# Expert weights in units of 2 MB instead of 1 MB, with shuffled row copies and a gather for two experts at a time

## The chip, the cores and the metric

One core of a Trainium2 chip runs the kernel. The metric is the device time of one execution, in microseconds (us); less is better.

## The reference

One layer: a mixer (gated linear attention beside a Mamba-2 state-space group) over 16 meta tokens and 256 tokens of width 1024, a LayerNorm, then a mixture of 32 experts, four for each token, and a last LayerNorm. The change is in the mixture, whose blocks hold the tokens of one expert:

```python
logits = (t @ router_w + router_b)
top_v, top_i = lax.top_k(logits, TOP_K)          # 4 of 32
gates = jax.nn.softmax(top_v, axis=-1)
...
xb = t_pad[tok]                                  # the tokens of expert e
hid = clamped_swiglu(xb @ w_gate[e] + b_gate[e], xb @ w_up[e] + b_up[e])
yb = hid @ w_down[e] + b_down[e]
...
out = jax.ops.segment_sum(yb * gate, row_tok)
```

All is float32. Each of w_gate, w_up and w_down is 1024 x 1024 per expert, 4 MB (of 1048576 bytes), so 12 MB per expert and 384 MB in all; every byte is read once.

## The kernel before, in words

The engines' programs are written out by hand, one function per engine, and tied by semaphores. SP issues nearly all loads, in the order of its program.

**Weights.** `ring` holds 16 slots of 1 MB. A unit is 256 rows of one matrix: partition p has rows 2p and 2p+1 side by side, so one partition gets 8 KB that are contiguous in HBM (`unit_src`, L241; `slot`, L248). An expert has 12 units (UPE), in the order w_gate, w_up, w_down. During the mixer the ring holds the 12 units of w_in and four of w_out, in packets of 256 columns (1 KB); as TensorE is through with them (`w_used`, L299), SP fills their slots with expert 0's units and four of expert 1's. Four further units, the w_gate of expert 28, go to the `spare` tiles (`load_spare`, L302) once their places in `arena` are free, and the last round of the ring skips them (`ring_at`, L258). From then on SP waits for each unit until the one 16 before it is used, and issues it (L329). Rounds are of four experts (UNROLL); the rounds between first and last are a loop.

**A tile** is one expert with up to 64 of its tokens (SL). DVE (`select`, L1260) builds `sel`, a 0/1 matrix of tokens by slots, `selG`, the same with the gates' weights, and `oh`. TensorE gathers (`gather`, L930): for each of eight row groups of 128 (`pair_rows`, L254) and two tiles of tokens it multiplies 128 columns of `xh` (as weights, column step two, since rows 2p and 2p+1 lie in one partition) with 64 columns of `sel`. ACT copies the result to `xT`. `hidden` (L947 to L961) multiplies xT with the units of w_gate into bank 4, then w_up into bank 5; the two halves of 512 columns go to two halves of the array. DVE and ACT make the clamped SwiGLU (L1290 to L1299) in `u_c`, TensorE transposes it (L975), and multiplies with w_down (L990). The output goes back to the tokens by `scatter` (L942), with the transposed selG, into banks 0 to 3, which hold the sum over all experts; `start_sums` (L917) begins them with the bias b_down, `add_residual` (L925) adds the residual before the last round. In a tile the first half of the previous tile's scatter stands between w_gate and w_up, then after w_up the gather of the next expert, the transposes of u_c and of selG, and the scatter's second half. Experts with over 64 tokens would get further tiles in a loop at the end; there are none in the profile.

Each `mm` on float32 is two instructions in the profile. The count of a row of TensorE is thus twice that of the code.

Of the kernel before, what the change touches and what calls it, by code (L numbers as in the profile page):

```python
# [8 lines left out]
ALU = mybir.AluOpType  # L9
# [31 lines left out]
RING = 16  # L41
UW = 2048
UPE = 3 * D * FF // (P * UW)
UNROLL = 4
ROUNDS = NE // UNROLL
SPARE = 4
# [9 lines left out]
def build(nc, x, meta, ln_in_g, ln_in_b, w_in, gla_w_a2, gla_b_a, gla_norm_g, ssd_conv_w, ssd_conv_b,  # L56
          ssd_dt_bias, ssd_a_log, ssd_d, ssd_norm_g, w_out, ln1_g, ln1_b, router_w, router_b,
          w_gate, w_up, b_gate, b_up, w_down, b_down, ln2_g, ln2_b, out):
    with ExitStack() as ctx:
# [7 lines left out]
        arena = sb("arena", [P, 19392])  # L67
# [56 lines left out]
        spare = [cut(at, 2, D) for at in (8320, 16576, 3072, 5248)]  # L124
        xT = [cut(at, KT, SL) for at in (2048, 12672)]
# [7 lines left out]
        sel = cut(7808, 2, NT, SL)  # L133
        selGT = cut(10880, SEQ)
# [67 lines left out]
        ln1_in, ln2_in, bias_in, late_in, out_done = sem("ln1_in"), sem("ln2_in"), sem("bias_in"), sem("late_in"), sem("out_done")  # L202
        landed = [sem(f"landed{s}") for s in range(RING)]
# [37 lines left out]
        def unit_src(e, u):  # L241
            m = (w_gate, w_up, w_down)[u // (UPE // 3)]
            q = u % (UPE // 3)
            rows = slice(q * 2 * P, (q + 1) * 2 * P)
            return m[0, e, rows, :].rearrange("(p k) n -> p (k n)", k=2) if isinstance(e, int) else \
                m[0, bass.ds(e, 1), rows, :].rearrange("a (p k) n -> p (a k n)", k=2)

        def slot(s):  # L248
            return ring[:, s, :].rearrange("p (k n) -> p k n", k=2)
# [4 lines left out]
        def pair_rows(v, kt):  # L254

            return v.rearrange("p (q s k) -> p q k s", s=P, k=2)[:, kt // 2, kt % 2, :]
# [10 lines left out]
        def _(sp):  # L267
# [9 lines left out]
            for n, c0 in enumerate(W_ORDER):  # L277
                sp.dma_start(ring[:, n, :].rearrange("p (k n) -> p k n", k=KT),
                             w_in[0, :, c0:c0 + 256].rearrange("(k p) n -> p k n", p=P)).then_inc(landed[n], 16)
# [14 lines left out]
            for n in range(4):  # L294
                sp.dma_start(ring[:, U_OUT + n, :].rearrange("p (k n) -> p k n", k=KT),
                             w_out[0, :, 256 * n:256 * n + 256].rearrange("(k p) n -> p k n", p=P)).then_inc(landed[U_OUT + n], 16)
# [5 lines left out]
            def load_spare(q):  # L302
                sp.dma_start(unit_dst(spare[q]), unit_src(NE - UNROLL, q)).then_inc(spare_in, 16)

            def experts(it):
                first = isinstance(it, int) and it == 0
                for i in range(UPE * UNROLL):
# [6 lines left out]
                    if first and i == U_OUT:  # L314

                        sp.wait_ge(mixT_ps, 4)
                        load_spare(0)
                        sp.wait_ge(bparts_ok, 1)
                        load_spare(1)
                    if first and before < 0:  # L320
                        sp.wait_ge(*w_used[i])
                    else:
                        k, u = before // UPE, before % UPE
                        m, q = u // 4, u % 4
                        if q == 3:
                            sp.wait_ge((g_ps, u_ps, d_ps)[m], it * UNROLL + (k + 1))
                        else:
                            sp.wait_ge(unit_used, (it * UNROLL + k) * 9 + (3 * m + q + 1))
                    sp.dma_start(ring[:, at % RING, :], unit_src(it * UNROLL + i // UPE, i % UPE)).then_inc(landed[at % RING], 16)  # L329
                    if first and i == RING - 1:  # L330
                        sp.wait_ge(logit_ps, 1)
                        load_spare(2)
                        sp.wait_ge(h1_ok, NT)
                        load_spare(3)
# [4 lines left out]
            sp.wait_ge(g_ps, NE - UNROLL + 1)  # L339
# [18 lines left out]
        def _(pool):  # L358
# [54 lines left out]
            for t in range(NT):  # L413
                pool.wait_ge(h1T_ps, 2 * t + 2)
                link(nc.gpsimd.tensor_tensor(xh[:, t, :], xh[:, t, :], lnbc[:, 0, :], ALU.mult))
                nc.gpsimd.tensor_tensor(xh[:, t, :], xh[:, t, :], lnbc[:, 1, :], ALU.add).then_inc(h1_ok, 1)

        @block.scalar
        def _(act):
# [147 lines left out]
            def xT_evac(n, par, done):  # L567

                act.wait_ge(gath_ps, n + 1)
                if done is not None:  # L570
                    act.wait_ge(u_ps, done)
                nc.scalar.activation(xT[par][:, :, :].rearrange("p k s -> p (k s)"), bank[7][:, :], ACT.Copy).then_inc(xT_ok, 1)  # L572

            def tile(n, par, first, ahead):
                act.wait_ge(a_ok, n + 1)
                nc.scalar.activation(s_c, a_c, ACT.Sigmoid, scale=SALPHA).then_inc(sig_ok, 1)  # L576
                if ahead:
                    xT_evac(n + 1, 1 - par, None if first else n)
# [4 lines left out]
                act.wait_ge(selT_ps, n + 1)  # L583
                if not first:
                    act.wait_ge(scat[1], n)
                nc.scalar.activation(selGT, bank[5][:, 0:SEQ], ACT.Copy).then_inc(selGT_ok, 1)

            xT_evac(0, 0, None)
            for k in range(UNROLL):
                tile(k, k % 2, k == 0, True)  # L590
            with act.Fori(1, ROUNDS - 1) as it:
                for k in range(UNROLL):
                    tile(it * UNROLL + k, k % 2, False, True)
            for k in range(UNROLL):
                tile(NE - UNROLL + k, k % 2, False, k < UNROLL - 1)
            act.wait_ge(list_ok, 1)
            nx = act.value_load(xcount[0:1, 0:1], min_val=0, max_val=MAXX)
            with act.If(nx > 0):
                with act.Fori(0, nx) as i:
                    xT_evac(i + NE, 0, i + NE)  # L600
                    tile(i + NE, 0, False, False)
# [7 lines left out]
        def _(pe):  # L609
# [9 lines left out]
            def wslot(n, kt, a=0, b=256):  # L619
                return ring[:, n, :].rearrange("p (k n) -> p k n", k=KT)[:, kt, a:b]  # L620
# [32 lines left out]
            for c in range(XC):  # L653
                n = U_XBC + c // 2
                pe.wait_ge(landed[n], 16)
# [30 lines left out]
            pe.wait_ge(landed[U_K], 16)  # L686
# [15 lines left out]
            pe.wait_ge(landed[U_V], 16)  # L702
# [28 lines left out]
            pe.wait_ge(landed[U_V + 1], 16)  # L731
# [25 lines left out]
            pe.wait_ge(landed[U_Q], 16)  # L757
# [36 lines left out]
            for hf in range(2):  # L794
                n = U_Z + hf
                pe.wait_ge(landed[n], 16)
# [45 lines left out]
            for hf in range(2):  # L842
                n = U_OG + hf
                pe.wait_ge(landed[n], 16)
# [12 lines left out]
            def out_part(t, kts, first):  # L857
                for nb in range(2):
                    b = bank[((1, 4), (2, 3))[t][nb]]
                    for kt in kts:  # L860
                        ins = mm(b[:, :], mixT[:, kt, t * P:(t + 1) * P],  # L861
                                 ring[:, U_OUT + 2 * nb:U_OUT + 2 * nb + 2, kt * 256:(kt + 1) * 256],
# [4 lines left out]
            for n in range(4):  # L867
                pe.wait_ge(landed[U_OUT + n], 16)
# [51 lines left out]
            def add_residual():  # L920

                pe.wait_ge(residual_ok, 1)
                for t in range(NT):
                    for h in range(2):
                        mm(bank[2 * t + h][:, :], residual[:, :], xh[:, t, h * 512:(h + 1) * 512], start=False, stop=False,  # L925
# [11 lines left out]
            def scatter(n, t):  # L937
# [3 lines left out]
                for h in range(2):  # L941
                    ins = mm(bank[2 * t + h][:, :], selGT[h * SL:(h + 1) * SL, t * P:(t + 1) * P], y_s[h * SL:(h + 1) * SL, :],  # L942
# [3 lines left out]
            def tile(n, par, first, unit_at, arrived, gathers, scatters):  # L946

                def hidden(m, b, free, done):
# [5 lines left out]
                    for q in range(4):  # L954
                        arrived(4 * m + q)
                        for k in range(2):
                            kt = 2 * q + k
                            for h in range(2):
                                ins = mm(b[h * SL:(h + 1) * SL, :], xT[par][:, kt, :], unit_at(4 * m + q)[:, k, h * 512:(h + 1) * 512],  # L959
                                         start=False, stop=kt == KT - 1)  # L960
                        ins.then_inc(done if q == 3 else unit_used, 1)  # L961

                pe.wait_ge(selG_ok, n + 1)
                pe.wait_ge(xT_ok, n + 1)
                hidden(0, bank[4], a_ok, g_ps)
                if scatters:
# [411 lines left out]
```

## Time and profile before

| | |
|---|---|
| median of 3 runs | 1138.41 us (1137.51 to 1139.66) |
| the profiled execution | 1139.48 us |
| its span, first to last instruction | 1137.6 us |
| mean granted TensorE clock | 0.984 |
| TensorE (PE) busy | 1095.9 us, 96% |
| VectorE (DVE) / ScalarE (ACT) / GpSimd (POOL) busy | 231.1 / 123.7 / 30.7 us |
| DMA | 426.96 MB, 375 GB/s over the span |

The time of an execution contains the span and some 2 us around it. The page cuts the span in 40 slices of 28.4 us; digits are tenths busy. "PEld" is the load of TensorE's weights, which overlaps matmuls. In the chain of waits each piece is what the end was waiting for at that time. A matmul's end is modelled, so that consecutive rows of TensorE are best compared by their starts.

### The profile page before, as it was taken

To read this page: it belongs to the slowest core of one execution; us is meant where nothing else is said; L and a number is where in the kernel's file an instruction comes from. 1 tells how busy PE (TensorE), PEld (TensorE's weight loads), DVE (VectorE), ACT (ScalarE), POOL (GpSimd) and SP (SyncE) were. 2 spreads that over 40 slices of the span, in tenths; PEclk is the share of its full clock that TensorE was granted. 3 is DMA by queue.
4 is the path that set the end of the run, shared out by engine and by line. 5 is a ranking of instruction groups with operands and counts; after the bars stand their busy time and mean duration, and the time that the engine had idled before them with its cause. 6 is when DMAs were issued, how large, how long until landed. Compare 5 with 4: busy or idle time off the path is not lost.

```text
span 1137.6 us, 13806 instructions
## 1 busy us (share of the span) xinstructions
PE 1095.9 (96%) x5600; PEld 517.9 (46%) x5600; DVE 231.1 (20%) x528; ACT 123.7 (11%) x250; POOL 30.7 (3%) x37
## 2 busy tenths in 40 slices
PE   6999998999999999999999999999999999999994
PEld 5787756444444444444444433333333333344441
DVE  4422464011111111111111111111111111111114
ACT  2241422000000000000000000000000000000001
POOL 0230002000000000000000000000000000000000
PEclk9989997899999999999999999999999999999998
DMA  8973534899999999999999999999999999999992
GB/s 260 353 302 125 170 150 157 349 411 422 421 421 420 421 421 422 421 422 421 422 422 422 422 422 422 421 423 421 422 421 423 421 422 422 422 422 421 422 419 87
DMA packets 78240, 426.96 MB, mean 375 GB/s; under 512 B 10537, under 2 KB 27026, under 8 KB 29058
## 3 DMA queue, kind: packets, MB, share of 16 engines
q1 hardware_dynamic: 76082, 423.83, 91.4%
q10 hardware_dynamic: 2128, 2.70, 0.9%
q8 instruction: 22, 0.36, 0.1%
q14 instruction: 8, 0.07, 0.0%
HBM read 425.46 MB, written 1.05 MB: 375 GB/s over the span
## 4 chain that ended last, share of the span: by engine, by line
PE 66%; DMA 29%; DVE 2%; ACT 2%; SPq 1%; issue 0%; DVEq 0%
DMA ring<-in_moe_w_up 28%; PE bank L959 26%; PE bank L990 13%; PE bank L934 7%; PE bank L942 4%; PE bank L659 3%; PE bank L861 2%; PE bank L847 1%; PE bank L799 1%; SPq L329 1%; PE bank L953 1%; PE bank L975 1%; PE bank L735 1%; PE bank L675 1%; PE bank L761 1%; PE bank L682 0%
## 5 line engine op out<-in xcount | busy, mean ns | idle before, releaser
L959 PE MATMUL bank<-ring,arena 128*64 128x512 f32 x2016 | 452.7, 596 | 13.6 <-DMA ring<-in_moe_w_up 13.6
L959 PEld LDWEIGHTS bank<-ring,arena 128*64 128x64 f32 x2016 | 139.7, 137 | 294.4 <-issue 234.5
L990 PE MATMUL bank<-ring,arena 128*64 128x512 f32 x1024 | 231.1, 604 | 0.0
L990 PEld LDWEIGHTS bank<-ring,arena 128*64 128x64 f32 x1024 | 71.7, 139 | 156.2 <-issue 137.0
L934 PEld LDWEIGHTS bank<-arena 128*128 128x128 f32 x1024 | 126.2, 200 | 25.1 <-issue 25.1
L934 PE MATMUL bank<-arena 128*128 128x64 f32 x1024 | 130.4, 287 | 0.0
L1303 DVE COPY arena<-bank 128x512 f32<-128x512 f32 x32 | 22.1, 692 | 346.3 <-PE bank L990 346.3
L1294 DVE TENSOR_SCALAR arena<-bank 128x512 f32<-128x512 f32 x32 | 22.1, 692 | 261.9 <-PE bank L959 261.9
L942 PE MATMUL bank<-arena 64*128 64x512 f32 x256 | 72.2, 642 | 0.9 <-DVE arena L1303 0.9
L576 ACT ACTIVATE arena<-arena 128x512 f32<-128x512 f32 x32 | 20.2, 631 | 465.8 <-DVE arena L1290 465.8
L1290 DVE TENSOR_SCALAR arena<-bank 128x512 f32<-128x512 f32 x32 | 22.1, 692 | 186.9 <-PE bank L959 186.9
L572 ACT ACTIVATE arena<-bank 128x512 f32<-128x512 f32 x32 | 19.1, 598 | 362.1 <-PE bank L934 362.1
L942 PEld LDWEIGHTS bank<-arena 64*128 64x128 f32 x256 | 19.4, 184 | 32.5 <-issue 32.5
L659 PE MATMUL bank<-arena,ring 128*128 128x272 f32 x128 | 30.4, 393 | 0.7 <-ACT arena L436 0.7
L861 PE MATMUL bank<-ring,arena 128*128 128x512 f32 x64 | 27.9, 593 | 0.9 <-ACT arena L430 0.9
L953 PE MATMUL bank<-arena 96*64 96x512 bf16 x128 | 25.7, 396 | 0.8 <-ACT arena L572 0.8
L659 PEld LDWEIGHTS bank<-arena,ring 128*128 128x128 f32 x128 | 23.8, 190 | 5.5 <-ACT arena L436 0.9
L975 PE MATMUL bank<-ident,arena 128*128 128x128 f32 x128 | 21.7, 292 | 2.2 <-DVE arena L1299 2.2
L1299 DVE SCALAR_TENSOR_TENSOR arena<-arena 128x512 f32<-128x512 f32 x32 | 22.2, 693 | 3.3
L953 PEld LDWEIGHTS bank<-arena 96*64 96x64 bf16 x128 | 7.3, 108 | 34.0 <-issue 34.0
L1296 DVE TENSOR_TENSOR arena<-arena 128x512 f32<-128x512 f32 x32 | 21.8, 681 | 0.0
L975 PEld LDWEIGHTS bank<-ident,arena 128*128 128x128 f32 x128 | 19.1, 218 | 3.1 <-DVE arena L1299 3.1
(242 smaller groups left out, 527.0 us busy)
## 6 DMA issues: line engine op xcount, KB each, us to landing
ring<-in_moe_w_up SPq DMA_DIRECT2D x128, 1024.0 KB, 26.2
ring<-in_moe_w_down SPq DMA_DIRECT2D x128, 1024.0 KB, 26.3
ring<-in_moe_w_gate SPq DMA_DIRECT2D x124, 1024.0 KB, 25.7
ring<-in_w_in SPq DMA_DIRECT2D x12, 1024.0 KB, 11.9
ring<-in_w_out SPq DMA_DIRECT2D x4, 1024.0 KB, 13.7
arena<-in_moe_w_gate SPq DMA_DIRECT2D x4, 1024.0 KB, 4.7
arena<-in_x SPq DMA_DIRECT2D x2, 512.0 KB, 4.7
arena<-in_ln_in_g SPq DMA_DIRECT2D x1, 512.0 KB, 10.0
```

The costliest lines, as they stand in the source:

```text
L659: ins = mm(bank[4 + c % 3][:, 3:3 + TOK], wslot(n, kt, (c % 2) * P, (c % 2) * P + P), hT[:, kt, :], start=kt == 0, stop=kt == KT - 1)
L861: ins = mm(b[:, :], mixT[:, kt, t * P:(t + 1) * P], ring[:, U_OUT + 2 * nb:U_OUT + 2 * nb + 2, kt * 256:(kt + 1) * 256], start=first and k ...
L934: ins = mm(bank[7][:, kt * SL:(kt + 1) * SL], pair_rows(xh[:, t, :], kt), sel[:, par, t, :], start=t == 0, stop=t == 1)
L942: ins = mm(bank[2 * t + h][:, :], selGT[h * SL:(h + 1) * SL, t * P:(t + 1) * P], y_s[h * SL:(h + 1) * SL, :], start=False, stop=False, ski ...
L953: mm(b[h * SL:(h + 1) * SL, :], oh[:, par, :], bparts[:, m, h * 512:(h + 1) * 512], start=True, stop=False)
L959: ins = mm(b[h * SL:(h + 1) * SL, :], xT[par][:, kt, :], unit_at(4 * m + q)[:, k, h * 512:(h + 1) * 512], start=False, stop=kt == KT - 1)
L975: ins = tr(bank[4][:, c * P:(c + 1) * P], pair_rows(u_c, c), ident[:, :])
L990: ins = mm(bank[6][h * SL:(h + 1) * SL, :], hidT[:, kt % 4, (kt // 4) * SL:(kt // 4 + 1) * SL], unit_at(8 + q)[:, k, h * 512:(h + 1) * 512 ...
L1290: ts(a_c, bank[4][:, :], LIMIT, None, ALU.min).then_inc(a_ok, 1)
L1294: ts(u_c, bank[5][:, :], LIMIT, -LIMIT, ALU.min, ALU.max).then_inc(u_ok, 1)
L1299: stt(u_c, u_c, 1.0, a_c, ALU.add, ALU.mult).then_inc(hid_ok, 1)
L1303: copy(y_s, bank[6][:, :]).then_inc(yd_ok, 1)
```

## The change

A unit becomes 512 rows of one matrix, 2 MB: partition p has rows 4p to 4p+3, 16 KB contiguous in HBM. The ring has 8 such slots, an expert 6 units (two per matrix). The spares are six pieces of 1 MB (8 KB in a partition) instead of four: w_gate and half of w_up of expert 28, the first in a place of its own and loaded at once behind w_out.

With four rows per partition, a row group would take every fourth column. To keep the step at two, POOL writes the normalised tokens to a new tile `h1p` in a shuffled order (per block of 512: two halves, each with two neighbours of four), and DVE writes `a_c` and `u_c` in the same order. `add_residual` reads h1p back in natural order.

The gather is made for two experts at once: `sel` has 64 columns of each, and a gather of 4 row groups with 128 columns stands in each of two tiles: tile n makes half of what experts n+2 and n+3 (n even) or n+1 and n+2 (n odd) need. The halves go to `xA` (two buffers) and `xB`. So both halves for experts 0 and 1 come first, and experts 30 and 31 gather nothing. The transposes of selG move ahead of w_up and into bank 6, `selGT` gets two buffers, the scatter's first half moves behind w_up, and start_sums ahead of w_up. The scratch for descriptors that software makes shrinks to 1024 bytes, which gives room in SBUF.

```diff
-RING = 16
-UW = 2048
+RING = 8
+UW = 4096
+HW = UW // 2
+RPP = UW // FF
 UPE = 3 * D * FF // (P * UW)
+UPM = UPE // 3
-SPARE = 4
+SPARE = 3
...
-        arena = sb("arena", [P, 19392])
+        arena = sb("arena", [P, 19392 + NT * D + HW])
...
-        spare = [cut(at, 2, D) for at in (8320, 16576, 3072, 5248)]
-        xT = [cut(at, KT, SL) for at in (2048, 12672)]
+        h1p = cut(19392, NT, D)
+        spare = [cut(at, 2, D) for at in (19392 + NT * D, 8320, 16576, 3072, 5248, 0)]
+        xA = [cut(at, 4, 2 * SL) for at in (2048, 11648)]
+        xB = cut(12672, 4, 2 * SL)
...
-        sel = cut(7808, 2, NT, SL)
-        selGT = cut(10880, SEQ)
+        sel = cut(7808, NT, 2 * SL)
+        selGT = [cut(at, SEQ) for at in (10880, 16320)]
...
+            m, q = (w_gate, w_up, w_down)[u // UPM], u % UPM
+            rows = slice(q * RPP * P, (q + 1) * RPP * P)
+            return m[0, e, rows, :].rearrange("(p k) n -> p (k n)", k=RPP) if isinstance(e, int) else \
...
+        def shuffled(v):
+            return v.rearrange("p (q a s k) -> p q a s k", a=2, s=P, k=2)
+        def natural(v):
+            return v.rearrange("p (q s a k) -> p q a s k", a=2, s=P, k=2)
+        def row_group(v, kt):
+            return shuffled(v)[:, kt // RPP, kt % RPP // 2, :, kt % 2]
...
-            w_used = [(conv_ps, 2), (conv_ps, 4), (conv_ps, 6), (conv_ps, 8), (k_ps, 1), (v_ps, 3), (v_ps, 3), (q_ps, 1),
-                      (half_used, 1), (z_ps, 2), (half_used, 2), (og_ps, 2), (wout_ps, 3), (wout_ps, 3), (wout_ps, 4), (wout_ps, 4)]
+            w_used = [((conv_ps, 4),), ((conv_ps, 8),), ((k_ps, 1), (v_ps, 3)), ((q_ps, 1),), ((z_ps, 2),), ((og_ps, 2),),
+                      ((wout_ps, 3),), ((wout_ps, 4),)]
+            load_spare(0)
...
-                nc.gpsimd.tensor_tensor(xh[:, t, :], xh[:, t, :], lnbc[:, 1, :], ALU.add).then_inc(h1_ok, 1)
+                for q in range(2):
+                    ins = nc.gpsimd.tensor_tensor(shuffled(h1p[:, t, :])[:, q, :, :, :], natural(xh[:, t, :])[:, q, :, :, :],
+                                                  natural(lnbc[:, 1, :])[:, q, :, :, :], ALU.add)
+                ins.then_inc(h1_ok, 1)
...
-            def gather(n, par):
-                pe.wait_ge(sel_ok, n + 1)
-                for kt in range(KT):
+            def gather(g, pair, half, b):
+                pe.wait_ge(sel_ok, pair + 1)
+                for k in range(4):
                     for t in range(NT):
-                        ins = mm(bank[7][:, kt * SL:(kt + 1) * SL], pair_rows(xh[:, t, :], kt), sel[:, par, t, :], start=t == 0, stop=t == 1)
+                        ins = mm(b[:, k * P:(k + 1) * P], row_group(h1p[:, t, :], 4 * half + k), sel[:, t, :], start=t == 0, stop=t == 1)
                 ins.then_inc(gath_ps, 1)
...
-                ts(u_c, bank[5][:, :], LIMIT, -LIMIT, ALU.min, ALU.max).then_inc(u_ok, 1)
+                ts(shuffled(u_c)[:, 0, :, :, :], natural(bank[5][:, :])[:, 0, :, :, :], LIMIT, -LIMIT, ALU.min, ALU.max).then_inc(u_ok, 1)
```

**TensorE, the tile of expert 1.** In these names L953 and L982 are the bias of w_gate and w_up, L959 and L988 those matrices, L942 and L971 half a scatter, L934 and L963 the gather, L975 and L1009 the transposes of u_c, L978 and L997 those of selG, L990 and L1020 w_down. Before:

```order
L953 MATMUL bank<-arena 64x512 x2
L959 MATMUL bank<-ring,arena 64x512 x16
L942 MATMUL bank<-arena 128x512 x2
L953 MATMUL bank<-arena 64x512 x2
L959 MATMUL bank<-ring,arena 64x512 x16
L934 MATMUL bank<-arena 128x64 x16
L975 MATMUL bank<-ident,arena 128x128 x4
L978 MATMUL bank<-ident,arena 128x128 x2
L942 MATMUL bank<-arena 128x512 x2
L990 MATMUL bank<-ring,arena 64x512 x16
```

and now:

```order
L982 MATMUL bank<-arena 64x512 x2
L988 MATMUL bank<-ring,arena 64x512 x16
L997 MATMUL bank<-ident,arena 128x128 x2
L982 MATMUL bank<-arena 64x512 x2
L988 MATMUL bank<-ring,arena 64x512 x16
L971 MATMUL bank<-arena 128x512 x2
L963 MATMUL bank<-arena 128x128 x8
L1009 MATMUL bank<-ident,arena 128x128 x4
L971 MATMUL bank<-arena 128x512 x2
L1020 MATMUL bank<-ring,arena 64x512 x16
```

The gather has half the instructions at twice the columns; the selG transposes and half a scatter have changed sides of w_up.

**TensorE, the last tile** from its bias of w_up on (the same names). Before:

```order
L953 MATMUL bank<-arena 64x512 x2
L959 MATMUL bank<-ring,arena 64x512 x16
L975 MATMUL bank<-ident,arena 128x128 x4
L978 MATMUL bank<-ident,arena 128x128 x2
L942 MATMUL bank<-arena 128x512 x2
L990 MATMUL bank<-ring,arena 64x512 x16
```

and now, where the tile before it (expert 30) reads the same:

```order
L982 MATMUL bank<-arena 64x512 x2
L988 MATMUL bank<-ring,arena 64x512 x16
L971 MATMUL bank<-arena 128x512 x2
L1009 MATMUL bank<-ident,arena 128x128 x4
L971 MATMUL bank<-arena 128x512 x2
L1020 MATMUL bank<-ring,arena 64x512 x16
```

Without a gather, half a scatter is all that stands between w_up and the transposes, in two tiles now.

**SP, from the loads of w_out to the end of expert 1's units** (L303 and L322 are the spares). Before:

```order
L295 DMA ring<-in_w_out 128x8x256 x4
L329 DMA ring<-in_moe_w_gate 128x2048 x4
L329 DMA ring<-in_moe_w_up 128x2048 x4
L329 DMA ring<-in_moe_w_down 128x2048 x4
L303 DMA arena<-in_moe_w_gate 128x2048 x2
L329 DMA ring<-in_moe_w_gate 128x2048 x4
L303 DMA arena<-in_moe_w_gate 128x2048 x2
L329 DMA ring<-in_moe_w_up 128x2048 x4
L329 DMA ring<-in_moe_w_down 128x2048 x4
```

and now:

```order
L315 DMA ring<-in_w_out 128x8x256 x4
L322 DMA arena<-in_moe_w_gate 128x2048
L351 DMA ring<-in_moe_w_gate 128x4096 x2
L351 DMA ring<-in_moe_w_up 128x4096 x2
L351 DMA ring<-in_moe_w_down 128x4096 x2
L322 DMA arena<-in_moe_w_gate 128x2048 x2
L351 DMA ring<-in_moe_w_gate 128x4096 x2
L322 DMA arena<-in_moe_w_gate 128x2048
L322 DMA arena<-in_moe_w_up 128x2048 x2
L351 DMA ring<-in_moe_w_up 128x4096 x2
L351 DMA ring<-in_moe_w_down 128x4096 x2
```

Half as many issues of twice the size, and two more pieces to the spares.

## Rows read from the trace of the kernel before

**Rows 1.** The page: GB/s in 40 slices, and the packets.
```profile
GB/s 260 353 302 125 170 150 157 349 411 422 421 421 420 421 421 422 421 422 421 422 422 422 422 422 422 421 423 421 422 421 423 421 422 422 422 422 421 422 419 87
DMA packets 78240, 426.96 MB, mean 375 GB/s; under 512 B 10537, under 2 KB 27026, under 8 KB 29058
```

**Rows 2.** The page: the chain that ended last, by engine and by line.
```profile
PE 66%; DMA 29%; DVE 2%; ACT 2%; SPq 1%; issue 0%; DVEq 0%
DMA ring<-in_moe_w_up 28%; PE bank L959 26%; PE bank L990 13%; PE bank L934 7%; PE bank L942 4%; PE bank L659 3%; PE bank L861 2%; PE bank L847 1%; PE bank L799 1%; SPq L329 1%; PE bank L953 1%; PE bank L975 1%; PE bank L735 1%; PE bank L675 1%; PE bank L761 1%; PE bank L682 0%
```

**Rows 3.** The chain in order of time: start, duration, what.
```profile
340.26 6.87 PE bank L959 x32
...
368.33 6.87 PE bank L959 x32
...
467.68 3.91 PE bank L934 x32
...
843.86 27.01 DMA ring<-in_moe_w_up
...
903.49 27.01 DMA ring<-in_moe_w_up
```

**Rows 4.** Timeline of TensorE, expert 27: start, duration, instruction, idle before.
```profile
992.66 1.94 PE L959 MATMUL bank<-ring,arena 128*64 128x512 f32 x8 [0.55 <-DMA ring<-in_moe_w_up]
994.53 3.98 PE L934 MATMUL bank<-arena 128*128 128x64 f32 x32
998.35 0.68 PE L975 MATMUL bank<-ident,arena 128*128 128x128 f32 x4
998.86 0.38 PE L978 MATMUL bank<-ident,arena 128*128 128x128 f32 x2
999.17 1.13 PE L942 MATMUL bank<-arena 64*128 64x512 f32 x4
1000.23 7.09 PE L990 MATMUL bank<-ring,arena 128*64 128x512 f32 x32
```

**Rows 5.** Timeline of SP's queue: the first refills, and the first of w_down's slots.
```profile
196.92 5.48 SPq L329 DMA_DIRECT2D ring<-in_moe_w_up  x4
...
221.51 6.62 SPq L329 DMA_DIRECT2D ring<-in_moe_w_gate  x4
```

**Rows 6.** Windows: stretch, busy us by engine, granted clock, DMA share, GB/s.
```profile
30.00:46.00 16.00, 16.00 (x78) 13.22 (x77) 8.25 (x16) 2.98 (x11) 3.05 (x4) 1.00 1.10 348
300.00:900.00 600.00, 590.82 (x3045) 246.55 (x3044) 91.35 (x209) 44.63 (x84) 0.00 (x0) 1.00 1.01 422
188.00:192.00 4.00, 4.00 (x21) 4.00 (x21) 0.00 (x0) 0.00 (x0) 0.00 (x0) 0.50 0.00 0
216.00:224.00 8.00, 8.00 (x20) 2.17 (x20) 0.00 (x0) 0.00 (x0) 0.00 (x0) 0.57 0.47 177
224.00:232.00 8.00, 8.00 (x40) 2.64 (x38) 1.69 (x6) 0.00 (x0) 0.00 (x0) 1.00 0.99 361
```

**Rows 7.** Timeline of all engines, from the second LayerNorm to the first gather.
```profile
168.22 2.13 PE L617 MATMUL bank<-ident 128*128 128x128 f32 x18
...
178.44 2.35 POOL L416 TENSOR_TENSOR arena<-arena 128x1024 f32<-128x1024 f32 x1
...
184.65 0.42 DVE L1271 TENSOR_SCALAR arena<-arena 128x64 f32<-128x64 f32 x2
...
185.57 6.93 PE L934 MATMUL bank<-arena 128*128 128x64 f32 x32
```

**Rows 8.** The page's costliest groups: the gather's weight loads, count, busy us, mean ns.
```profile
L934 PEld LDWEIGHTS bank<-arena 128*128 128x128 f32 x1024 | 126.2, 200 | 25.1 <-issue 25.1
```

**Rows 9.** Timeline of TensorE, the last expert, from w_up on.
```profile
1103.60 7.03 PE L959 MATMUL bank<-ring,arena 128*64 128x512 f32 x32
...
1112.83 0.75 PE L975 MATMUL bank<-ident,arena 128*128 128x128 f32 x4 [2.19 <-DVE arena L1299]
...
1115.00 8.51 PE L990 MATMUL bank<-ring,arena 128*64 128x512 f32 x32
```

More of the change, by code:

```diff
@@ L202, in build @@
         ln1_in, ln2_in, bias_in, late_in, out_done = sem("ln1_in"), sem("ln2_in"), sem("bias_in"), sem("late_in"), sem("out_done")
+        w_landed = [sem(f"w_landed{n}") for n in range(16)]
         landed = [sem(f"landed{s}") for s in range(RING)]
@@ L963, in tile @@
                 pe.wait_ge(selG_ok, n + 1)
-                pe.wait_ge(xT_ok, n + 1)
-                hidden(0, bank[4], a_ok, g_ps)
-                if scatters:
-                    scatter(n - 1, 0)
+                hidden(0, bank[4], hidT_ok, g_ps)
+                if not first:
+                    pe.wait_ge(yd_ok, n)
+                for t in range(NT):
+                    ins = tr(bank[6][:, t * P:(t + 1) * P], selG[:, par, t, :], ident[:, :])
+                ins.then_inc(selT_ps, 1)
@@ L968, in tile @@
                 if first:
+                    start_sums()
                     pe.wait_ge(list_ok, 1)
                 hidden(1, bank[5], u_ok, u_ps)
-                if gathers:
-                    gather(n + 1, 1 - par)
+                if scatters:
+                    scatter(n - 1, 0, 1 - par)
+                if gathers is not None:
+                    gather(*gathers, bank[7])
                 pe.wait_ge(hid_ok, n + 1)
                 for c in range(4):
-                    ins = tr(bank[4][:, c * P:(c + 1) * P], pair_rows(u_c, c), ident[:, :])
+                    ins = tr(bank[4][:, c * P:(c + 1) * P], row_group(u_c, c), ident[:, :])
@@ L1002, in arrived @@
                         if at is None:
-                            pe.wait_ge(spare_in, 16 * SPARE)
+                            pe.wait_ge(spare_in, 16 * 2 * SPARE)
                         else:
-                            pe.wait_ge(landed[at % RING], it * (UPE * UNROLL // RING * 16) + (2 + at // RING) * 16)
+                            pe.wait_ge(landed[at % RING], it * (UPE * UNROLL // RING * 16) + (1 + at // RING) * 16)
                     n = it * UNROLL + k
-                    first, last = (isinstance(n, int) and n == m for m in (0, NE - 1))
-                    tile(n, k % 2, first, unit_at, arrived, not last, not first)
+                    first = isinstance(n, int) and n == 0
+                    ahead = not (isinstance(n, int) and n >= NE - 2)
+                    pe.wait_ge(xT_ok, n + 2 if ahead else NE)
+                    tile(n, k % 2, first, unit_at, arrived, k // 2,
+                         (n + 2, it * (UNROLL // 2) + (k // 2 + 1), k % 2) if ahead else None, not first)
             pe.wait_ge(h1_ok, NT)
-            gather(0, 0)
+            gather(0, 0, 0, bank[7])
+            pe.wait_ge(GT_ok, 1)
+            gather(1, 0, 1, bank[6])
             pe.wait_ge(bparts_ok, 1)
@@ L1019, in _ @@
             for t in range(NT):
[L1020 removed]
+                scatter(NE - 1, t, 1)
             pe.wait_ge(list_ok, 1)
@@ L1284, in _, with tile @@
             copy(xcount, rank[:, 3 * NE - 1:3 * NE]).then_inc(list_ok, 1)
-            def tile(n, par, first, after):
+            def tile(n, par, first, after, pair):
+                if pair is not None:
+                    select(n + 2, pair)
                 if after is not None:
-                    select(None if first else n, after, 1 - par)
+                    weigh(None if first else n, after, 1 - par)
                 dve.wait_ge(g_ps, n + 1)
-                ts(a_c, bank[4][:, :], LIMIT, None, ALU.min).then_inc(a_ok, 1)
+                ts(shuffled(a_c)[:, 0, :, :, :], natural(bank[4][:, :])[:, 0, :, :, :], LIMIT, None, ALU.min).then_inc(a_ok, 1)
                 dve.wait_ge(u_ps, n + 1)
```

202 lines of the change are left out of this document (105 added, 97 removed).

## The prediction

> **What bounds the kernel now.** Read the page first. The rate of the DMA engines is the flattest line on it: 421 to 423 GB/s from the eleventh slice to the thirty-eighth [rows 1], while TensorE looks just as full. The two can't both be the limit, so the chain of waits comes next: 28% of the span is a wait for a w_up unit, and TensorE has 66% [rows 2]. In order of time it has three parts. Early, the w_gate phase of one expert starts 28.07 us after the last (340.26 to 368.33): TensorE's own pace. From about 635 us the chain is DMA, and two experts take 903.49 - 843.86 = 59.63 us, 29.82 us each [rows 3]. At 994.53 us, when the last w_up unit of expert 27 is used, it goes back to TensorE, because expert 28 finds its w_gate in the spare units [rows 4].
>
> Why does the rate not fall while TensorE sets the pace? An expert needs 12.58 MB. At 28.07 us that is 448 GB/s, more than DMA delivers; the full 16 MB ring is being eaten up and is empty at 635 us. So from 221.5 us on, when SP issues the first refill of a w_down unit [rows 5], transfers never stop, and what counts is **rate x bytes up to expert 27's last w_up, then TensorE's work after it**. Faster work of TensorE before that point only empties the ring sooner.
>
> **The packet.** From 300 to 900 us packets of 8 KB (two rows of 4 KB in a partition) run at 422 GB/s; from 30 to 46 us the w_in packets of 1 KB run at 348 [rows 6]. For one of 16 engines that is 310.6 ns for 8 KB and 47.1 ns for 1 KB. A line through both: 9.4 ns for each packet, and 36.8 ps per byte (27.2 GB/s per engine, 435 for 16). A 16 KB packet would take 9.4 + 602.3 = 611.7 ns, 428.5 GB/s. One MB (1048576 bytes) then takes 2.447 us where it took 2.485.
> The Trainium skill (DMA: Bandwidth & Descriptors, Specifications) gives 435 GB/s as the ceiling of the ports into SBUF, which is where my line ends; its HBM limit per core there, about 358 GB/s, is refuted by the 422 of this trace, and by it longer packets would gain nothing.
>
> **The change, part by part.** Everything is against the profiled execution: 1137.6 us of span in 1139.48 us, the runs' median 1138.41.
> 1. *Longer packets.* Units 24 to 331 (counted in MB from the first expert) pass between 221.5 us and expert 27's last w_up: 308 MB x (2.485 - 2.447) = **-11.7 us**. Bounds: 0 (the rate of 8 KB stays), and 308 x (2.485 - 2.410) = -23 us with no overhead at all. I take the line, since it comes out of two rates of this queue.
> 2. *When the stream becomes dense.* This is the first w_down release of expert 0. Sel for two experts adds two DVE operations of 64 columns, +0.4 us, ahead of the first gather [rows 7]. Both first gathers together have 32 instructions, as the 6.93 us of now, 217 ns each at half the clock; with 128 columns at most twice the 118 of a transpose (5), 236 ns or +0.6 us, and I take nothing. In tile 0 the gather is half, -1.95 us (see 5), of which the DVE chain to hid_ok takes back 0.2. The first release comes after 2 MB, not 1: 1.75 us more at full clock, and with the granted clock at 0.57 from 216 to 224 us [rows 6] up to 3.4. The four matmuls with b_down only move from behind the transposes to ahead of w_up. Together +1.8 us (range 0.4 to 2.7). Against it, the 1 MB refills ran dry while TensorE was slow: 361 GB/s from 224 to 232 us [rows 6], which is 1.2 us lost; two 2 MB refills bridge this. Net **+0.7 us**, with -0.8 to +2.7 as bounds.
> 3. *The last w_up unit is twice as large.* After it lands TensorE has 16 instructions instead of 8, 3.6 us instead of the 1.9 from 992.66 [rows 4]: **+1.7 us**.
> 4. *From there to expert 27's w_down.* Before, 994.53 to 1000.23 [rows 4]. Now the transposes of selG (998.86 to 999.17, 0.31 us) stand ahead of w_up, the first half of the scatter (1.06 us, 999.17 to 1000.23) comes here from ahead of w_up, and the gather has 16 instructions of 128 columns instead of 32 of 64.
> 5. *The gather's price.* The 32 take 3.82 us until the transposes (994.53 to 998.35) and 3.9 on the chain, 122 ns each [rows 3, 4]. A weight load of 128x128 is recorded with 200 ns, but they overlap [rows 8]; a matmul of 64 columns is the shorter part of the pair. With 128 columns behind each load there are 18 transposes in 2.13 us, 118 ns each [rows 7]. So 16 x 122 ns = 1.95 us, a gain of 1.95. Worst: 16 x 200 = 3.2, a gain of 0.7. I take 1.95, as the transposes have the same load and the same columns. Term 4 is then -1.95 - 0.3 + 1.06 = **-1.2 us**.
> 6. *Experts 28 to 31, TensorE's pace.* 28 and 29 still gather: -1.95 each; the part moved inside a tile nets to nothing. 30 no longer gathers, and now waits for DVE's chain as 31 does: w_down came 5.7 us after w_up with a gather and 4.4 without (1110.63 to 1115.00) [rows 9], so -1.3, -0.3 for the selG transposes that stood there, and -0.75 for 0.31 instead of 1.06 between w_gate and w_up: -2.3. Expert 31: -0.3 and -0.75, -1.05. Sum **-7.3 us**. It holds only if DMA isn't behind: expert 27's last w_up lands at 992.6 - 11.7 + 0.7 = 981.6; the 4 MB of its w_down and the 42 left take 46 x 2.447 = 112.6 us, to 1094.2. TensorE's last w_down ends at 1115.0 + 8.5 - 17.8 = 1105.7 and wants its last 2 MB 3.5 us before, at 1102.2: 8 us of cover. The two more MB in spares are 4.9 of these 8 and earn nothing else.
> 7. *Costed at nothing.* POOL writes t=1's rows in two strided pieces of 512; it ended at 180.8 and the gather started at 185.57 [rows 7], so even twice the 2.35 us is hidden; without that cover it costs its own excess. w_in and w_out land in halves of slots, same bytes. The first fill waits for two units' users, but DMA stands idle from 188 to 192 us and on to 196.92, when the first refill is issued [rows 5, 6]. DVE's two strided writes read PSUM in pairs: before 635 us they lie under the gather and the scatter, in 30 and 31 not; 10% more is 0.1 us. After the last w_down nothing changes.
>
> Sum: -11.7 + 0.7 + 1.7 - 1.2 - 7.3 = **-17.8 us**, so 1138.4 - 17.8 = **1120.6 us**.
>
> **Rivals.** A measurement of this kernel can tell about 0.2%, 2.3 us.
> *A, the packets bring no rate.* Either the 3% between 422 and 435 is not per packet, or the queue cuts a row of 16 KB in two. For it: only two points make the line, and the packets of 1 KB are strided reads. Against: 422 is the same in TensorE's part and in DMA's, so nothing but the transfers themselves sets it. Then the sum is -6.1: 1132.3 us, faster by TensorE's end alone.
> *B, long reads are slower.* Packets that are under way at the same time lie twice as far apart in HBM; if they then get in each other's way, the rate falls. In -6.1 + 308 x d the sum passes +2.3 at d = 0.027 us per MB, that is under 417.4 GB/s; at 413 (2.539) it is -6.1 + 16.6 = +10.5, 1149 us. For it: the 1 KB reads of w_in also lay apart by whole rows of w_in and were slow, which the line lays to their size alone. Against: the unit as a whole is as contiguous as before.
> [...]
> *C, TensorE's clock falls in new gaps.* At 1115 us w_down took 8.51 us against 7.09 after a gap of 2.2 us [rows 4, 9]. Tiles 30 and 31 now both have a gap, but of 1.1 us, as half a scatter stands in it. Two falls: +1.4 us on mine, 1122; none: 1119.2. It is inside the forecast.
> *D, partly.* A third or two thirds of the rate: 1124 to 1129.
>
> **How the numbers follow.** Forecast with C 0.66 (the line through two rates is good evidence, the trace has no 16 KB packet); A 0.18; D 0.10; B and any other unseen loss, such as a queue that runs dry with eight slots, 0.06. The range must take in A, and below it the no-fall case and a somewhat better rate: 1116 to 1133.5. The forecast's own range is 1117 to 1124. A and D are still faster by over 0.2% (1136.1). So faster 0.93, same 0.03, slower 0.04.
>
> **What would show it.** Packets of 8 KB and more fall by half, from 78240 - 29058 = 49182 [rows 1]. The windows from 300 to 900 us read 428, not 422; DMA waits on the chain start earlier: the ring's lead lasted 414 us at a loss of 1.75 us per expert, and at 29.4 - 26.1 = 3.3 it ends near 430 us. Matmuls of the gather take 122 ns each, half as many. After expert 27's last w_up the chain is TensorE alone, in tiles of 26.1. A rate of 422 with this end speaks for A, one under 418 for B; DMA waits in experts 28 to 31 would refute term 6.

## The result and the profile after

The changed kernel takes 1120.09 us (median of 4 runs, 1117.96 to 1121.48) against 1137.96 us beside it (4 runs, 1136.51 to 1139.66): ratio 0.9841, 95% interval 0.9819 to 0.9862. Forecast were 1120.6 us and a range from 1116.0 to 1133.5. Run again later (e9), the ratio was 0.9839 (0.9815 to 0.9863).

The first profile has a span of 1116.2 us in an execution of 1117.96 us, the quickest of the four, while the profile of the kernel before lies among its slow ones (1139.48 us). The two spans are thus 21.4 us apart, the medians 17.9. Its GB/s and packets, as in [rows 1], and the chain, as in [rows 2], on the page:

```profile
GB/s 260 353 319 151 129 164 237 312 426 426 428 427 426 429 427 428 429 427 429 429 429 428 428 428 430 428 429 428 428 429 427 429 429 429 428 428 428 428 427 103
DMA packets 51022, 426.93 MB, mean 382 GB/s; under 512 B 7513, under 2 KB 24002, under 8 KB 26034
...
PE 54%; DMA 40%; DVE 3%; ACT 2%; issue 1%; DVEq 0%; SPq 0%
```

TensorE is still 93% busy, and still isn't the bound: DMA has gone from 29 to 40% of the chain. 51022 - 26034 = 24988 packets of 8 KB or more moved what 49182 did. The windows, to set beside [rows 6]:

```profile
184.00:196.00 12.00, 10.50 (x63) 7.57 (x63) 4.49 (x22) 2.85 (x4) 0.00 (x0) 0.86 0.37 154
216.00:224.00 8.00, 7.27 (x36) 3.24 (x38) 0.00 (x0) 1.02 (x2) 0.00 (x0) 1.00 0.95 377
300.00:900.00 600.00, 561.50 (x2722) 209.54 (x2720) 92.21 (x212) 41.72 (x84) 0.00 (x0) 1.00 1.01 428
```

428 GB/s where 422 stood. And the chain in order of time (start, duration, what), as [rows 3]:

```profile
409.10 6.89 PE bank L988 x32
416.01 34.16 DMA ring<-in_moe_w_up
...
590.94 35.41 DMA ring<-in_moe_w_up
...
679.03 35.41 DMA ring<-in_moe_w_up
...
943.31 35.41 DMA ring<-in_moe_w_up
```

The chain goes over to DMA at 416 us, not at 635. From there a step of 679.03 - 590.94 = 88.09 us is three experts (36 MB): 2.447 us per MB, 29.36 per expert. The end of that stretch, on TensorE's timeline, as [rows 4]:

```profile
978.77 3.65 PE L988 MATMUL bank<-ring,arena 128*64 128x512 f32 x16 [1.24 <-DMA ring<-in_moe_w_up]
982.35 1.13 PE L971 MATMUL bank<-arena 64*128 64x512 f32 x4
983.41 2.15 PE L963 MATMUL bank<-arena 128*128 128x128 f32 x16
985.40 0.63 PE L1009 MATMUL bank<-ident,arena 128*128 128x128 f32 x4
985.96 1.13 PE L971 MATMUL bank<-arena 64*128 64x512 f32 x4
987.02 7.09 PE L1020 MATMUL bank<-ring,arena 128*64 128x512 f32 x32
994.03 3.89 PE L953 MATMUL bank<-arena,tri 128*128 128x512 f32 x8
997.86 0.41 PE L982 MATMUL bank<-arena 96*64 96x512 bf16 x2
...
1017.30 7.09 PE L1020 MATMUL bank<-ring,arena 128*64 128x512 f32 x32
...
1043.65 7.09 PE L1020 MATMUL bank<-ring,arena 128*64 128x512 f32 x32
...
1095.00 7.09 PE L1020 MATMUL bank<-ring,arena 128*64 128x512 f32 x32
```

After 978.77 there is no wait for DMA up to the end, as in the kernel before. The difference of the spans, 1137.6 - 1116.2 = 21.4 us, falls to these stretches, each from a start to a start:

| stretch | before | after | difference | forecast |
|---|---|---|---|---|
| to the first w_down refill (SP) | 221.51 | 221.06 | -0.5 | +1.8 |
| from there to the last w_up of expert 27 | 771.2 | 757.7 | -13.4 | -11.7 - 1.2 |
| that unit's matmuls, to the next work | 1.9 | 3.6 | +1.7 | +1.7 |
| to expert 27's w_down | 5.7 | 4.7 | -1.0 | -1.2 |
| to expert 31's w_down | 114.8 | 108.0 | -6.8 | -7.3 |
| from there to the end | 22.6 | 21.2 | -1.4 | 0 |

In the profile of e9, an execution of 1121.45 us, the same rows come to +2.4, -12.8, then +0.7 for the next two together, -6.8 and -1.4, in all -17.9 us: between these two profiles the first row moves by 2.9 us, the second by 0.6 and the others by less than 0.1.

### The profile page after: what moved, and what is told of

Same layout as the page of the kernel before. It is cut to its first block, busy times and chain, and to the rows that moved or that the text cites. A ratio compares the mean times of both kernels' runs of the same rounds, so it can differ in the third digit from the quotient of the medians.

```text
span 1116.2 us, 12278 instructions
## 1 busy us (share of the span) xinstructions
PE 1040.0 (93%) x5088; PEld 457.1 (41%) x5088; DVE 231.6 (21%) x528; ACT 119.6 (11%) x250; POOL 31.9 (3%) x39
## 2 busy tenths in 40 slices
DMA packets 51022, 426.93 MB, mean 382 GB/s; under 512 B 7513, under 2 KB 24002, under 8 KB 26034
## 4 chain that ended last, share of the span: by engine, by line
PE 54%; DMA 40%; DVE 3%; ACT 2%; issue 1%; DVEq 0%; SPq 0%
DMA ring<-in_moe_w_up 22%; PE bank L988 20%; DMA ring<-in_moe_w_gate 18%; PE bank L1020 12%; PE bank L963 3%; PE bank L971 3%; PE bank L687 3%; PE bank L889 2%; PE bank L875 1%; PE bank L827 1%; PE bank L1009 1%; PE bank L763 1%; PE bank L982 1%; PE bank L789 1%; PE bank L703 1%
## 5 line engine op out<-in xcount | busy, mean ns | idle before, releaser
L988 PE MATMUL bank<-ring,arena 128*64 128x512 f32 x2000 | 452.0, 598 | 45.6 <-DMA ring<-in_moe_w_up 34.5
L988 PEld LDWEIGHTS bank<-ring,arena 128*64 128x64 f32 x2000 | 139.1, 137 | 328.1 <-issue 239.4
L1020 PE MATMUL bank<-ring,arena 128*64 128x512 f32 x1024 | 226.8, 595 | 0.7 <-issue 0.7
L1020 PEld LDWEIGHTS bank<-ring,arena 128*64 128x64 f32 x1024 | 71.1, 137 | 151.9 <-issue 151.9
L963 PEld LDWEIGHTS bank<-arena 128*128 128x128 f32 x512 | 64.0, 200 | 23.3 <-issue 23.3
L971 PE MATMUL bank<-arena 64*128 64x512 f32 x256 | 72.0, 640 | 0.9 <-DVE arena L1351 0.9
L963 PE MATMUL bank<-arena 128*128 128x128 f32 x512 | 69.9, 291 | 0.2 <-DVE arena L1310 0.2
L598 ACT ACTIVATE arena<-bank 128x512 f32<-128x512 f32 x32 | 19.1, 597 | 326.5 <-PE bank L963 326.5
L971 PEld LDWEIGHTS bank<-arena 64*128 64x128 f32 x256 | 19.4, 184 | 31.0 <-issue 27.3
L982 PE MATMUL bank<-arena 96*64 96x512 bf16 x128 | 25.7, 396 | 0.7 <-issue 0.7
L1009 PE MATMUL bank<-ident,arena 128*128 128x128 f32 x128 | 20.5, 283 | 2.4 <-DVE arena L1347 2.3
L612 ACT ACTIVATE arena<-bank 128x512 f32<-128x512 f32 x32 | 19.0, 593 | 18.0 <-PE bank L1009 18.0
L1009 PEld LDWEIGHTS bank<-ident,arena 128*128 128x128 f32 x128 | 17.7, 202 | 4.2 <-DVE arena L1347 4.2
## 6 DMA issues: line engine op xcount, KB each, us to landing
ring<-in_w_in SPq DMA_DIRECT2D x12, 1024.0 KB, 11.7
```

The lines of the kernel that those rows point to most:

```text
L963: ins = mm(b[:, k * P:(k + 1) * P], row_group(h1p[:, t, :], 4 * half + k), sel[:, t, :], start=t == 0, stop=t == 1)
L971: ins = mm(bank[2 * t + h][:, :], selGT[par][h * SL:(h + 1) * SL, t * P:(t + 1) * P], y_s[h * SL:(h + 1) * SL, :], start=False, stop=False ...
L982: mm(b[h * SL:(h + 1) * SL, :], oh[:, par, :], bparts[:, m, h * 512:(h + 1) * 512], start=True, stop=False)
L988: ins = mm(b[h * SL:(h + 1) * SL, :], (xA[pp], xB)[q][:, k, par * SL:(par + 1) * SL], unit_at(UPM * m + q, k)[:, h * 512:(h + 1) * 512], s ...
L1009: ins = tr(bank[4][:, c * P:(c + 1) * P], row_group(u_c, c), ident[:, :])
L1020: ins = mm(bank[6][h * SL:(h + 1) * SL, :], hidT[:, kt % 4, (kt // 4) * SL:(kt // 4 + 1) * SL], unit_at(2 * UPM + q, k)[:, h * 512:(h + 1) ...
```

## The experiments

All kernels below are the changed kernel with the edit shown. e1 to e4, e5 to e8, and e9 with e10 ran together, each group on one chip and beside its own runs of the kernel before. Differences to the changed kernel therefore go by ratios where nothing else is said.

### Is it the packet?

The theory is the line of the prediction: 9.4 ns per packet and 36.8 ps per byte on each of 16 engines. Three kernels change the packet (the spares stay at 8 KB), and with it the number of transfers: two or four for a unit, or one for two units. A fourth changes the number of transfers alone.

**e1_packets_8k**, and with `PARTS = 4` **e2_packets_4k**:

```diff
-                    sp.dma_start(ring[:, at % RING, :], unit_src(...)).then_inc(landed[at % RING], 16)
+                    for j in range(PARTS):                       # 2; part j: rows 4p+2j, 4p+2j+1
+                        w = UW // PARTS
+                        sp.dma_start(ring[:, at % RING, j * w:(j + 1) * w], part_src(..., j)).then_inc(landed[at % RING], 16)
...
```

> The changed kernel, but each ring unit of 2 MB is loaded by two DMAs of 8 KB per partition (rows 4p, 4p+1, then 4p+2, 4p+3). Slots, waits, layout and TensorE's work stay. Theory (a fixed price per packet): the windows from 300 to 900 us fall from 428 back to 422 GB/s, 2.485 us per MB, and the time rises by 308 x 0.038 = 11.7 us, to 1131.8. Rival (the gain of rate comes from fewer, larger units): 428 GB/s stays, 1120. Packets of 8 KB and more go back to about 49 thousand by both.

> As the one with packets of 8 KB, but four DMAs of 4 KB per partition for each ring unit. The line through 1 KB and 8 KB gives 9.4 + 150.6 = 160.1 ns per packet, 409 GB/s from 300 to 900 us and 2.561 us per MB: 308 x 0.114 = +35 us on the change, 1155. Rival (1 KB was slow for its strides and there is no price per packet from 4 KB on): 422 GB/s or more, at most 1132.

**e4_packets_32k**, a whole matrix into two slots, outside the last round:

```diff
+                    if paired:
+                        sp.dma_start(ring[:, (at - 1) % RING:(at - 1) % RING + 2, :].rearrange("p a n -> p (a n)"),
+                                     matrix_src(it * UNROLL + i // UPE, i % UPE // UPM)).then_inc(landed[(at - 1) % RING], 16)
...
```

> The changed kernel, but except in the last round a whole matrix of 4 MB is loaded by one DMA into two neighbouring slots, 32 KB per partition. The rows of a matrix then lie in other places than the tokens' columns (the output is not the layer's; the work is the same). The line gives 9.4 + 1204.6 = 1214 ns per packet, 432 GB/s, 2.428 us per MB: -5.7 us over some 300 MB. Against it, TensorE has 7.0 us instead of 3.6 to do after expert 27's w_up has landed (+3.4), and the first w_down is released 3.5 us later (+2 to +3.5): about 1120 to 1121.5 us in all, at 432 GB/s from 300 to 900 us. Rival (the gain ends at 16 KB): 428 GB/s and about 1126.

The window from 300 to 900 us of each (columns as in [rows 6]). e1_packets_8k, whose page counts 49181 packets of 8 KB or more, as before the change:

```profile
300.00:900.00 600.00, 552.74 (x2672) 205.26 (x2670) 90.22 (x209) 40.63 (x82) 0.00 (x0) 1.00 1.01 422
```

e2_packets_4k, with 98800 packets between 2 and 8 KB:

```profile
300.00:900.00 600.00, 536.41 (x2592) 198.15 (x2590) 87.49 (x200) 39.72 (x80) 0.00 (x0) 1.00 1.03 409
```

e4_packets_32k, with 14236 packets of 8 KB or more:

```profile
300.00:900.00 600.00, 568.58 (x2705) 212.92 (x2702) 91.35 (x211) 40.63 (x82) 0.00 (x0) 0.98 1.00 432
```

| packet | line | measured | time, expected | time, ratio to before (95%) |
|---|---|---|---|---|
| 4 KB | 409 | 409 GB/s | 1155 | 1155.58, 1.0150 (1.0119 to 1.0181) |
| 8 KB | 422 | 422 | 1131.8 | 1130.73, 0.9933 (0.9906 to 0.9960) |
| 16 KB (the change) | 428.5 | 428 | | 1120.09, 0.9841 |
| 32 KB | 432 | 432 | 1120 to 1121.5 | 1123.40, 0.9867 (0.9841 to 0.9894) |

Two points drew the line, and three that weren't there when it was drawn lie on it. With 8 KB the changed kernel gives back over half of its gain; what is left, 0.7% or 8 us, fits TensorE's end, reckoned at 6.1. Which bytes a unit has, their place in HBM and the slots are those of the change in e1, so neither the larger unit nor the distance of the rows made the rate. A price for each transfer is not yet ruled out by these four rows: from 4 to 32 KB the packets per MB (16, 8, 4, 2) and the transfers per MB (2, 1, 0.5, 0.25) fall together.

On the pages of e1 and e2 the chain names SP's queue (52 and 58%) where the change has DMA. SP's issuing did not set the rate of e1: the kernel before has the same 422 GB/s with the same packets and 1% of SPq in its chain, and in both experiments the engines were busy all the time (share 1.01 and 1.03).

At 32 KB the rate rose as expected and the time did not fall: 1123.4. By the ratio that is 1 to 3 us above the 1120 to 1121.5 expected, and not clear of the change (the intervals overlap). The first SP issue behind expert 0's w_down comes at 227.13 us, 3 to 7 us later than in the runs with 16 KB, and the matmuls of expert 27's w_up, ahead of which the wait had grown to 1.92 us, took 8.78 us instead of 7.09:

```profile
979.16 8.78 PE L1000 MATMUL bank<-ring,arena 128*64 128x512 f32 x32 [1.92 <-DMA ring<-in_moe_w_up]
```

The mean granted clock of this execution is 0.969, against 0.990 in the first profile of the change. Whether the clock fell there because of the wait was not tried by itself.

**e3_two_issues_16k** was to double the transfers and leave the packets:

```diff
+                    for j in range(PARTS):                       # 2 halves of the partitions
+                        w = P // PARTS
+                        sp.dma_start(ring[j * w:(j + 1) * w, at % RING, :], unit_src(...)[j * w:(j + 1) * w, :]).then_inc(landed[at % RING], 16)
...
```

> The changed kernel, but each ring unit of 2 MB is loaded by two DMAs of 64 partitions each, with packets of 16 KB as before. It doubles the transfers without touching the packets. Theory: 428 GB/s and 1120 us stay. Rival (the price belongs to each transfer and its completion, not to each packet): 422 GB/s and 1132 us.

Neither. It took 1970.94 us, ratio 1.727 (1.717 to 1.736):

```profile
300.00:900.00 600.00, 389.63 (x1342) 125.83 (x1340) 45.13 (x104) 19.86 (x40) 0.00 (x0) 0.80 1.01 218
```

Half of 435, with all 16 engines busy (share 1.01): a packet of 16 KB takes twice its time. The test thus says nothing on the price of a transfer. An estimate of it comes out of the other rows, with the w_in loads as the one row in which packets and transfers part: per MB and engine the w_in loads have 64 packets of 1 KB and one completion, the 4 KB kernel 16 and 2, the 8 KB one 8 and 1. From 1 KB to 8 KB (3.013 to 2.485 us per MB) 56 packets cost 0.528 us, 9.4 ns each; from 4 KB to 8 KB 8 packets and one completion cost 0.079 us, of which the packets are 0.075. A completion is left with 0.003 us, no more than what the rounding of the two rates to 1 GB/s makes of it, so it can't be told from nothing. This rests on the w_in row: its 1 KB reads are strided and come from the mixer's stage. Were they slow for that, packet and transfer could still share the price; no run here separates them at 8 or 16 KB.

### Is TensorE free in the middle?

**e5_gather_twice**: every gather inside a tile runs its eight matmuls twice.

> The changed kernel, but every gather inside a tile is done twice into the same bank (16 more instructions of 128 columns, 2.0 us of TensorE in each of 30 tiles; the result is the same). Theory (TensorE's work counts only before the stream is dense and after expert 27's last w_up): it shows in tiles 0, 27, 28 and 29 alone, +8 us, so about 1128, with 428 GB/s from 300 to 900 us. Rival (TensorE is the bound, as 93% busy says): +60 us, about 1180.

1129.08 us, ratio 0.9893 (0.9861 to 0.9924): 0.0052 or 6 us above the change. One of the four runs, at 1121.70, pulls the ratio down; by the medians it is 9 us above the change and 8 above e6, which ran beside it. TensorE's added 60 us have gone for the most part where it was idle, as the window shows:

```profile
300.00:900.00 600.00, 594.29 (x3068) 251.65 (x3068) 92.20 (x212) 41.71 (x84) 0.00 (x0) 1.00 1.01 428
```

and on TensorE's timeline

```profile
984.44 3.65 PE L988 MATMUL bank<-ring,arena 128*64 128x512 f32 x16 [0.91 <-DMA ring<-in_moe_w_up]
```

99% busy instead of 94%, the same 428 GB/s, still a wait of 0.9 us at expert 27's w_up. The chain goes over to DMA at 716 us here instead of 416: the slower TensorE only emptied the ring later. So the halved gather of the change is worth nothing in 26 of its 30 tiles. The rival's 60 us did not come.

### What do the spares earn?

**e6_spares_4mb** has `SPARE = 2` and leaves out the last two of six spare loads.

> The changed kernel with 4 MB of spares as before the change instead of 6 MB (w_gate of expert 28 alone). Theory: the two MB only widen DMA's cover at the end from 3 to 8 us, so nothing changes: 1120 us (within 1.5), and expert 28 starts its w_up without a wait or with one under 1 us. Rival (each MB loaded ahead takes its 2.45 us off the end): +4.9 us, 1125.

1121.27 us, ratio 0.9849 (0.9827 to 0.9870): the same as the change, and not 4.9 us more, though the interval would hold a part of it. Expert 28's w_up runs without a wait, as expected.

**e7_spares_for_26** and **e8_spares_for_25** keep the 6 MB and move their place:

```diff
-            if isinstance(it, int) and it == ROUNDS - 1:
-                return None if i < SPARE else i - SPARE
+            if isinstance(it, int) and it >= ROUNDS - 2:
+                g, s0 = it * UPE * UNROLL + i, SKIP * UPE        # SKIP = 26 or 25
+                if g >= s0:
+                    return None if g < s0 + SPARE else i - SPARE
...
-            with sp.Fori(1, ROUNDS - 1) as it:                   # PE's loop likewise
+            with sp.Fori(1, ROUNDS - 2) as it:
                 experts(it)
+            experts(ROUNDS - 2)
```

> The changed kernel, but the 6 MB of spares are the w_gate and half of the w_up of expert 26 instead of 28, so that TensorE's stretch after the last wait begins two experts sooner (the rounds of experts 24 to 31 stand outside the loop). Theory: until the spares DMA sets the pace with 29.4 us per expert, after them TensorE with 26.35, so each expert sooner takes 3.0 us off, 6.0 for two: 1114 us. Rival (the bytes are the same, so their place can't matter): 1120.

> As with the spares for expert 26, but for expert 25. Theory: TensorE's stretch would be 9.0 us shorter in all, but the last unit lands only 7.7 us before TensorE wants it in the changed kernel (1090.8 against 1098.5 us), so the gain stops there and DMA sets the end again, with a wait for w_down or w_up in experts 29 to 31: 1112 to 1113 us. If there were no such limit: 1111. Rival (the place can't matter): 1120.

1115.90 us, ratio 0.9782 (0.9757 to 0.9807), and 1115.15 us, ratio 0.9794 (0.9775 to 0.9813). The place matters: neither interval meets that of the change. Two experts earlier gives 4 us by the medians and 7 by the ratios (one run at 1108.35 pulls that one), where 6 were expected; against e6, beside it, it is 5. The third expert gives nothing more that can be told from noise, and 1115.15 is 2 us above the 1112 to 1113 expected. Expert 31 in the latter kernel's timeline shows why:

```profile
1073.40 3.65 PE L992 MATMUL bank<-ring,arena 128*64 128x512 f32 x16 [1.24 <-DMA ring<-in_moe_w_gate]
...
1083.19 3.65 PE L992 MATMUL bank<-ring,arena 128*64 128x512 f32 x16 [1.25 <-DMA ring<-in_moe_w_up]
1086.78 1.13 PE L975 MATMUL bank<-arena 64*128 64x512 f32 x4
...
1090.77 7.09 PE L1024 MATMUL bank<-ring,arena 128*64 128x512 f32 x32
```

TensorE waits for the last **w_up**, and w_down is there when it is wanted. Its w_down starts 4.2 us before the changed kernel's 1095.00, and 1.2 of these are a stream that became dense sooner (219.91 against 221.06 us; expert 0's w_up took 8.29 us there instead of 9.57, see step 2 below). So the last w_up leaves 3 us to be had, and by the later pair of profiles 5. In the kernel with the spares for expert 26 the same wait is there with 0.77 us.

Both again, beside the same runs of the kernel before:

> The changed kernel itself, on the same chip and beside the same runs of the kernel before as the next. Theory: 1120 to 1121 us, ratio 0.984. Its profile shows whether the start (the first refill of a w_down slot, 221.06 us in the profile so far) and the clock of the last w_down move from execution to execution: I expect the start to lie anywhere from 220 to 224 us.

> The kernel with the spares for expert 25 once more, now beside the changed kernel. After its first run the limit is known: the last w_up lands 4.4 us before the changed kernel wants it, so 4 to 5 us less than the changed kernel, about 1116, ratio 0.980. Rival (the first run's gain came from the chip or the run): no difference from the changed kernel.

1118.71 us, ratio 0.9839 (0.9815 to 0.9863), and 1115.95 us, ratio 0.9809 (0.9787 to 0.9831). The five runs of one lie between 1117.85 and 1121.45, those of the other between 1114.31 and 1116.37: no run of the two overlaps, 2.8 us by the medians. It beats both kernels, the changed one by somewhat less than the 4 to 5 us expected. The profile of the change was a slower one this time, span 1119.7 us, with the first w_down refill at 223.89 us where it had been 221.06:

```profile
149.35 20.77 PE L889 MATMUL bank<-ring,arena 128*128 128x512 f32 x48
...
223.89 0.33 SPq L351 DMA_DIRECT2D ring<-in_moe_w_gate  x1
...
982.27 3.65 PE L988 MATMUL bank<-ring,arena 128*64 128x512 f32 x16 [1.25 <-DMA ring<-in_moe_w_up]
```

The same 48 matmuls with w_out start at 146.57 in the first profile, so the 2.8 us arise in the mixer, which the change leaves alone; from the refill to the w_up it is 758.4 us (757.7). What comes late there comes late at the end.

## Why the prediction was right

The mechanism held: rate times bytes up to expert 27's last w_up, then TensorE alone. The sum held within the noise. That it came within 1 us is partly luck: the start alone moves by 4 us between profiles, a clock fall that was counted in did not come, and the start was wrong in its parts. Step by step:

1. **Longer packets, -11.7.** Right to the nanosecond that can be read: 2.447 us per MB was forecast and the chain has it. The stretch as a whole is 13.4 us shorter, 12.9 with the 1.2 us of refills that no longer run dry. The line through two rates was enough, and e1, e2 and e4 lie on it; that the price belongs to the packet and not to the transfer is argued from the w_in row, not shown by itself. The Trainium skill (DMA: Bandwidth & Descriptors, Bandwidth) has about 10.5 ns per packet from another kind of queue; this queue's 9.4 stands beside it.
2. **The start, +1.8.** Mis-sized, by 2.3 us in the first profile. I took over the half clock of the first gathers, 217 ns per instruction. The windows from 184 to 196 us say 0.86 here, 0.50 before, and the 32 instructions took 5.31 us instead of 6.93. Why the clock was up was not tried. The run-to-run spread of this very point is as large (219.91 to 223.93 us over the profiles at 16 KB with one gather), so no single profile could settle the term. Another part was wrong too: I had laid the low clock from 216 to 224 us on w_down and charged its second MB with up to 3.4 us. Before:

```profile
202.08 7.05 PE L959 MATMUL bank<-ring,arena 128*64 128x512 f32 x32
...
213.70 4.16 PE L917 MATMUL bank<-arena 32*128 32x512 f32 x8
217.79 9.97 PE L990 MATMUL bank<-ring,arena 128*64 128x512 f32 x32
```

and now:

```profile
199.46 4.31 PE L945 MATMUL bank<-arena 32*128 32x512 f32 x8
...
204.13 9.57 PE L988 MATMUL bank<-ring,arena 128*64 128x512 f32 x32
...
217.38 7.09 PE L1020 MATMUL bank<-ring,arena 128*64 128x512 f32 x32 [0.73 <-issue]
```

From 200 us on, the slow matmuls of both kernels are those that follow `start_sums` (L917, L945). The change moved it ahead of w_up, so that w_up is slow now (9.57 us instead of 7.05) and w_down is not (7.09 instead of 9.97; the clock from 216 to 224 us is 1.00). The first 2 MB of w_down are free 3.68 us after its start, where 1 MB took 3.72 before. Whether the clock falls because of `start_sums` was not tried.

3. **The larger last unit, +1.7.** 978.77 to 982.35 is 3.6 us, as said.
4. **To w_down, -1.2.** -1.0. The 16 instructions of the gather take 1.99 us (983.41 to 985.40), 124 ns each where 122 were forecast.
5. **Experts 28 to 31, -7.3.** -6.8. A tile took 1043.65 - 1017.30 = 26.35 us, not 26.1.
6. **The cover of 8 us** was the step that was wrong, and it cost nothing. I looked for the last unit of all, w_down. In the first profile it is issued at 1065.4 and lands 27.0 us later, 6 us ahead of its matmuls (1095.00 + 3.5), not 8. The last w_up has less: issued at 1057.9, it lands 24.8 us later, at 1082.7, and its matmuls start at 1087.5 (1084.03 + 3.4), 4.8 us behind. The kernels with the spares for expert 25 put it at 3 to 5 us. That the 2 MB more of spares earn nothing stands (e6).
7. **Costed at nothing.** POOL's two strided pieces take 2.95 us instead of 2.35 and end at 181.83, 4 us ahead of the gather. The residual's matmuls, which now read every fourth pair, take 3.83 us instead of 3.63 and I had not counted them.

Of the rivals, **A** (no rate) and **D** fell with the window's 428. **B** (long reads slow) fell with it, and more so with 432 at 32 KB. **C**: no fall, the last w_down has 7.09 us; forecast for that case 1119.2, against 1120.09 measured. In the first profile this is the -1.4 us of the table's last line. The 1.1 us gaps in tiles 30 and 31 didn't bring the clock down in any profile of the change, where a gap of 2.2 us had been followed by it. I had said that DMA's stretch begins near 430 us; it begins at 416.

On one sentence of the prediction: the 358 GB/s per core that the 422 refute are, by the Trainium skill (HBM Reference, Specifications (TRN2)), the share when both cores of a pair stream; for a core alone it names about 425. One core ran here, and its 428 and 432 lie a little above that too.

## What to carry to other kernels

Where a stream of weights never stops, find the last place at which compute waits for it and count separately before and after: before it only bytes, packets and the time at which the stream becomes dense matter, after it only compute, and work saved on the wrong side is worth nothing. Price packets by a line through two sizes that the trace already holds; packets and transfers must part in it if the two are to be told apart. And put what is loaded ahead where it begins the compute-bound end early enough that stream and compute finish together.

## What the hardware showed unexpectedly

Two transfers of 64 partitions each, one behind the other on a queue, run at 218 GB/s, although all 16 engines are busy and the packets are those of the 428. A cause in the kernel's order was not tried. The Trainium skill (SBUF — State Buffer, Door 1: The DMA port swizzle (why `[64,N]` ≈ `[32,N]`)) says that partitions 0 to 63 cover only 8 of 16 ports and gives about 218 GB/s for them. It says further (the same page, "Can I just issue two DMAs to hit both halves?") that a second transfer does not add the other half. The trace agrees, with 218.
